# Smaller weight slots, modulation in single k steps with the gates as columns, and transposed rows split and evicted two k tiles at a time, in a three-block float32 layer stack on one core

## The reference, cut to what matters

```python
u = rms_norm(h, norm_g); proj = u @ w_in            # even and odd layer
...
return h + y @ w_out
...
def rms_norm_2(x, g):
    y = xf * lax.rsqrt(jnp.mean(xf * xf, axis=-1, keepdims=True) + EPS)
...
def modulate(h, shift, scale):
    return h * (1 + scale) + shift
```

## Time and profile before

| | before |
|---|---|
| median of 3 runs | 1040.92 us |
| lowest, highest | 1040.67, 1043.06 us |
| profiled execution, its own time | 1042.01 us |
| its span, first to last instruction | 1040.2 us |
| PE busy | 937.6 us (90%) |
| DVE busy | 703.0 us (68%) |
| ACT busy | 475.2 us (46%) |
| mean granted TensorE clock | 0.959 |

### The profile page before, as it was taken

How to read it: one execution, slowest core, us unless ns; L and a number is a source line. 1 busy time by engine, 2 the same in 40 slices (tenths; PEclk the granted TensorE clock), 3 DMA queues, 4 the chain that set the end, 5 groups by cost and what they waited for, 6 DMA issues and landing times. The chain is left out here.

```text
span 1040.2 us, 14368 instructions
## 1 busy us (share of the span) xinstructions
PE 937.6 (90%) x5572; PEld 813.0 (78%) x5572; DVE 703.0 (68%) x1058; ACT 475.2 (46%) x800; POOL 66.9 (6%) x63
## 2 busy tenths in 40 slices
PE   4999988999798899999998989879989489999996
PEld 3788866989677778898988767776678389999885
DVE  4557787878877746757677786658854657754643
ACT  4455644554323335555564534334643434333441
POOL 0201101000000000201020000100001100000000
PEclk8999999899899879999999999989999889999999
DMA  7444364755566455444554575333222437753751
GB/s 266 162 163 145 127 215 161 239 191 187 179 218 217 149 202 163 165 148 158 180 168 142 184 253 194 129 122 122 82 82 81 142 100 243 249 193 108 241 204 41
DMA packets 89348, 174.55 MB, mean 168 GB/s; under 512 B 4269, under 2 KB 8770, under 8 KB 89282
## 3 DMA queue, kind: packets, MB, share of 16 engines
q1 hardware_dynamic: 86656, 166.78, 48.1%
q0 software_dynamic: 1888, 6.25, 1.9%
q10 hardware_dynamic: 738, 0.61, 0.2%
HBM read 172.57 MB, written 1.06 MB: 167 GB/s over the span
## 5 line engine op out<-in xcount | busy, mean ns | idle before, releaser
L1572 DVE TENSOR_TENSOR wlo<-raw,whi 128x1024 fp32r<-128x1024 f32 (+2 forms) x278 | 323.9, 1179 | 149.5 <-ACT whi L1289 148.6
L1289 ACT CAST whi<-raw 128x1024 fp32r<-128x1024 f32 (+2 forms) x278 | 276.7, 1011 | 201.8 <-PE acc L989 71.6
L998 PE MATMUL acc<-xhi,whi 128*128 128x256 f32 x736 | 214.3, 291 | 9.6 <-DVE slo L1590 4.6
L1000 PE MATMUL acc<-xlo,whi 128*128 128x256 f32 x736 | 209.6, 285 | 0.0
L999 PE MATMUL acc<-xhi,wlo 128*128 128x256 f32 x736 | 209.5, 285 | 0.0
L987 PE MATMUL acc<-whi,xhi 128*128 128x512 f32 (+2 forms) x368 | 150.4, 409 | 13.3 <-DVE xlo L1590 6.1
L998 PEld LDWEIGHTS acc<-xhi,whi 128*128 128x128 f32 x736 | 142.5, 194 | 13.0 <-issue 5.3
L989 PE MATMUL acc<-whi,xlo 128*128 128x512 f32 (+2 forms) x368 | 144.0, 391 | 0.0
L988 PE MATMUL acc<-wlo,xhi 128*128 128x512 f32 (+2 forms) x368 | 143.9, 391 | 0.0
L999 PEld LDWEIGHTS acc<-xhi,wlo 128*128 128x128 f32 x736 | 142.5, 194 | 0.7 <-issue 0.5
L1000 PEld LDWEIGHTS acc<-xlo,whi 128*128 128x128 f32 x736 | 142.4, 194 | 0.0
(11 more groups left out here) (291 smaller groups left out, 1175.2 us busy)
## 6 DMA issues: line engine op xcount, KB each, us to landing
raw<-in_e_w_in SPq DMA_DIRECT2D x28, 1024.0 KB, 5.3
raw<-in_o_w_in SPq DMA_DIRECT2D x28, 1024.0 KB, 5.1
raw<-in_w_mod SPq DMA_DIRECT2D x24, 1024.0 KB, 5.1
raw<-in_w_ffn_in SPq DMA_DIRECT2D x20, 1024.0 KB, 5.6
raw<-in_w_in SPq DMA_DIRECT2D x14, 1024.0 KB, 5.2
raw<-in_w_ffn_out SPq DMA_DIRECT2D x10, 1024.0 KB, 5.1
raw<-in_e_w_out SPq DMA_DIRECT2D x8, 1024.0 KB, 5.6
raw<-in_o_w_out SPq DMA_DIRECT2D x8, 1024.0 KB, 5.2
```

The lines of the kernel that those rows point to most:

```text
L998: mm(o, wh, hi, start=a, stop=False, skip_group_check=True)
L1000: last = mm(o, wh, lo, start=False, stop=z, skip_group_check=True)
L1289: nc.scalar.copy(whi[:, s.i % SPLIT_SLOTS, 0:s.nk, 0:n], raw[:, s.raw.i % RAW_SLOTS, s.koff:s.koff + s.nk, 0:n]).then_inc(S["hi_ready"], 1)
L1572: tt(wlo[:, slot, 0:s.nk, 0:n], raw[:, s.raw.i % RAW_SLOTS, s.koff:s.koff + s.nk, 0:n], whi[:, slot, 0:s.nk, 0:n].bitcast(F32), ALU.subtra ...
```

## The change

Raw weights lie in six slots of two k tiles, 512 KB each: the same memory, 326 loads in the place of 164. Modulation takes one k tile per position: one DVE instruction, or two for a ctx chunk, which has them at every second position; the wait for the step before stands at the head of the next. All chunks come out as columns, with the bias from a column; for a gate chunk DVE spreads the four columns over a diagonal (`gate_diag`), and one matmul with ones makes the row (`gate_rows`). The bias loads and `mod_bias` are gone. The chunks move: 0 to 3 now run from sub 12 to sub 82, 4 to 9 from sub 100 to sub 149, 10 and 11 from sub 216 to sub 233, their gate rows at 236 to 240. A sixth and seventh edit lie at the norms: `evac_resid` adds by row tile, with ACT's squares behind each (`mixsq`), so the norms after both layers need no pass over h; at the x norms DVE scales row tile 0 and ACT row tile 1, in two column halves; the 16 transposes come as four quarters of two k tiles, and with modulation ACT makes both xhi and scr from PSUM, DVE only the difference. POOL's load of the memory rows waits for the second raw slot. The memory rows (L1656 now) keep the old way of scaling.

```diff
-RAWK = 4
-RAW_SLOTS, SPLIT_SLOTS, LEAD = 3, 4, 3
+RAWK = 2
+RAW_SLOTS, SPLIT_SLOTS, LEAD = 6, 4, 3
...
-    def transposed(self, xn, ready, key, scale, bias=None):
-        for half in range(2):
-            st = self.step("rows_T", xn=xn, ready=ready, key=key, scale=scale, bias=bias, half=half)
+    def transposed(self, norm, key, scale, bias=None):
+
+        for q in range(4):
+            ready = [(n, norm.on[n] - 1 + q // 2 if norm.both else norm.on[n])
+                     for n in ("rows_ready", "rows_act") if n in norm.on]
+            st = self.step("rows_T", xn=norm.dst, ready=ready, key=key, scale=scale, bias=bias, q=q)
...
+    def mod(self, pos, chunk, ctx=False):
+
+        pos = max(pos, self.pos)
+        stride = 2 if ctx else 1
+
+        def read(k):
+            st = self.step("mod", chunk=chunk, u=k // RAWK, part=k % RAWK, ctx=ctx, prev=self.count.get("mod_read", 0),
+                           after=self.count.get("mod_ps", 0))
             self.tick(st, "mod_read")
...
+        last = pos + (KT - 1) * stride
+        for k in range(KT):
+            self.at(pos + k * stride, lambda k=k: read(k), 3)
+        self.at(last + 2, out, 2)
+        return last + (4 if ctx else 1)
...
-    m = pl.pos
-    for chunk in (6, 7, 8, 9, 0, 1, 2, 3):
-        m = pl.mod(m, chunk, ctx=chunk < 4)
...
+    m = pl.pos
+    for chunk in range(4):
+        m = pl.mod(m, chunk, ctx=True)
...
+    m = max(m, pl.pos + 4)
+    for chunk in range(4, 10):
+        m = pl.mod(m, chunk)
...
-    pl.mod(pl.mod(pl.pos + 4, 4, gate=True), 5, gate=True)
+    assert m <= pl.pos + 4, (m, pl.pos)
+    pl.gate_row(pl.gate_row(pl.pos + 4, 4), 5)
...
-    pl.mod(pl.mod(pl.pos + 8, 10, gate=True), 11, gate=True)
...
+    m = pl.mod(pl.mod(pl.pos + 8, 10), 11)
+    pl.gate_row(pl.gate_row(m + 4, 10), 11)
...
+                if st.both:
+                    wait(("rstd_ready", st.on["rstd_ready"]))
+                    for c in (slice(0, CW), slice(CW, D)):
+                        f(rows_of[st.dst][:, 1, c], rows_of[st.src][:, 1, c], ACT.Copy, scale=stat(st, 2)[:, 1:2])\
+                            .then_inc(S["rows_act"], 1)
+
+            def rows_T(st):
+                hi = (xhi if st.key == "x" else shi)[:, 2 * st.q:2 * st.q + 2, :]
+                wait(("rt_ps", st.on["rt_ps"]))
+                a = scale_cols(st.scale)
+                if st.bias is None:
+                    for k in range(2):
+                        kk = 2 * st.q + k
+                        last = f(hi[:, k, :], acct(st.acc)[:, kk % 4, :], ACT.Copy, scale=a[:, kk:kk + 1])
+                    last.then_inc(S["rt_hi"], 1)
+                    return
+                wait(("mcol_done", st.ready_cols))
+                b = scale_cols(st.bias)
+                tmp = scr[:, st.q % 2 * CW:st.q % 2 * CW + CW].rearrange("p (k t) -> p k t", t=T)
+                for dst in (hi, tmp):
+                    if dst is tmp:
+                        wait(st.free["scr"] if st.q == 0 else ("rt_lo", st.on["rt_lo"] - 2))
+                    for k in range(2):
+                        kk = 2 * st.q + k
+                        last = f(dst[:, k, :], acct(st.acc)[:, kk % 4, :], ACT.Identity, scale=a[:, kk:kk + 1],
+                                 bias=b[:, kk:kk + 1])
+                last.then_inc(S["rt_hi"], 1)
+
+            def evac_resid(st):
+                wait(st.free["scr"])
                 for t in range(NT):
+                    wait(("resid_done", st.on["resid_done"] - 1 + t))
+                    if t == 1:
+                        wait(("sq_ready", st.on["sq_ready"] - 1))
+                    f(scr[:, 0:CW], h_res[:, t, st.c * CW:(st.c + 1) * CW], ACT.Square,
+                      accum_out=mixsq[:, st.c, t:t + 1]).then_inc(S["sq_ready"], 1)
 
...
+            def panels_rstd(st, done):
+
+                wait(("sq_ready", done[0].on["sq_ready"]))
+                link(ts(stat(st, 0)[:, 0:NT], mixsq[:, 0, :], 1.0 / D, EPS, ALU.mult, ALU.add))
+                wait(("sq_ready", done[1].on["sq_ready"]))
+                stt(stat(st, 1)[:, 0:NT], mixsq[:, 1, :], 1.0 / D, stat(st, 0)[:, 0:NT], ALU.mult, ALU.add)\
+                    .then_inc(S["ms_ready"], 1)
+                wait(("rstd_ready", st.on["rstd_ready"]))
+
...
+                dst, src = rows_of[st.dst], rows_of[st.src]
+                if st.both:
+                    for c in (slice(0, CW), slice(CW, D)):
+                        ts(dst[:, 0, c], src[:, 0, c], stat(st, 2)[:, 0:1], None, ALU.mult).then_inc(S["rows_ready"], 1)
+                    return
...
-                b = scale_cols(st.bias)
-                tmp = scr[:, :].rearrange("p (k t) -> p k t", t=T)
-                wait(("rt_ps", st.on["rt_ps"]))
-                wait(st.free["scr"])
-                for k in range(4):
-                    last = ts(tmp[:, k, :], acct(st.acc)[:, k, :], a[:, k0 + k:k0 + k + 1],
-                              b[:, k0 + k:k0 + k + 1], ALU.mult, ALU.add)
-                last.then_inc(S["rt_tmp"], 1)
+                tmp = scr[:, st.q % 2 * CW:st.q % 2 * CW + CW].rearrange("p (k t) -> p k t", t=T)
                 wait(("rt_hi", st.on["rt_hi"]))
                 tt(lo, tmp, hi.bitcast(F32), ALU.subtract).then_inc(S["rt_lo"], 1)
...
-                half = RAWK // 2
-                for k in range(st.part * half, st.part * half + half):
-                    for v in range(2 if st.ctx else 1):
-                        c = scol[:, 8 * v + RAWK * st.u + k:8 * v + RAWK * st.u + k + 1]
-                        src = raw[:, st.raw.i % RAW_SLOTS, k, :]
-                        if st.u == 0 and k == 0:
-                            ins = ts(macc[:, v, :], src, c, None, ALU.mult)
-                        else:
-                            ins = stt(macc[:, v, :], src, c, macc[:, v, :], ALU.mult, ALU.add)
-                        if k % half == half - 1 and v == (1 if st.ctx else 0):
-                            ins.then_inc(S["mod_read"], 1)
-                            wait(("mod_read", st.on["mod_read"]))
-                        elif v == (1 if st.ctx else 0):
-                            link(ins)
-
-            def mod_bias(st):
-                wait(("bias_in", 16 * st.on["bias_in"]))
-                tt(macc[0:1, 0, :], macc[0:1, 0, :], macc[0:1, 1, :], ALU.add).then_inc(S["bias_done"], 1)
-
-            def mod_out(st):
+                wait(("mod_read", st.prev))
+                k = RAWK * st.u + st.part
+                if k == 0:
+                    wait(("mod_ps", st.after))
+                src = raw[:, st.raw.i % RAW_SLOTS, st.part, :]
+                for v in range(2 if st.ctx else 1):
+                    c = scol[:, 8 * v + k:8 * v + k + 1]
+                    m = macc[:, v if st.ctx else st.chunk % 2, :]
+                    if k == 0:
+                        ins = ts(m, src, c, None, ALU.mult)
+                    else:
+                        ins = stt(m, src, c, m, ALU.mult, ALU.add)
+                ins.then_inc(S["mod_read"], 1)
+
+            def mod_take(st):
+                st = st.first
                 wait(("mod_ps", st.on["mod_ps"]))
                 c = st.chunk
-                if st.gate:
-                    which = c >= 6
-                    dve.wait_ge(S["loaded_post_ffn" if which else "loaded_post_mix"], 16)
-                    g = post_gain[which][:, (c % 2) * CW:(c % 2 + 1) * CW]
-                    tt(g, tp[:, :], g, ALU.mult).then_inc(S["mod_sb"], 1)
-                    return
                 for v in range(2 if st.ctx else 1):
                     last = tt(modc[:, v, 4 * c:4 * c + 4], opsum[:, 4 * v:4 * v + 4],
                               cols[:, ROW["b_mod"] + 4 * c:ROW["b_mod"] + 4 * c + 4], ALU.add)
                 last.then_inc(S["mod_sb"], 1)
 
+            def gate_diag(st):
+                c = st.chunk
+                wait(("mod_sb", c + 1))
+                d = macc[:, c % 2, :].rearrange("p (i n) -> p i n", i=4)
+                tt(d, ident.unsqueeze(1).to_broadcast([P, 4, P]),
+                   modc[:, 0, 4 * c:4 * c + 4].unsqueeze(2).to_broadcast([P, 4, P]), ALU.mult).then_inc(S["gate_diag"], 1)
+
+            def gate_rows(st):
+                c = st.chunk
+                dve.wait_ge(S["loaded_post_ffn" if c >= 6 else "loaded_post_mix"], 16)
+                wait(("gate_ps", st.on["gate_ps"]))
+                g = post_gain[c >= 6][:, (c % 2) * CW:(c % 2 + 1) * CW]
+                tt(g, tp[:, :], g, ALU.mult).then_inc(S["gate_sb"], 1)
...
+            def load_mem(st):
+                pool.wait_ge(S["raw_loaded1"], 16)
+                pool.dma_start(h_res[:, :, :], w["mem"].rearrange("b (t p) d -> p (b t) d", p=P))\
+                    .then_inc(S["loaded_h"], 16)
```

More of the change, by code:

```diff
@@ L433, in load @@
         return st
-    def mod(self, pos, chunk, ctx=False, gate=False):
-        pos = max(pos, self.pos) + max(pos, self.pos) % 2
-        def read(u, part):
-            if u == 0 and part == 0 and gate:
```

(52 more changed lines are left out.)

176 lines of the change are left out of this document (97 added, 79 removed).

## The result

| | before | after |
|---|---|---|
| median (4 runs each, beside one another) | 1041.99 us | 1031.51 us |
| lowest, highest | 1040.67, 1045.24 | 1030.55, 1033.49 |
| profiled execution, span | 1042.01, 1040.2 | 1032.34, 1030.5 |
| mean granted TensorE clock | 0.959 | 0.956 |

The account below looks back on a forecast made before the run. TensorE was taken to bound the forgetting heads; elsewhere its waits on DVE's queue and the norm chains, with half-clock spells, were the loss. Terms summed to -32.8: 1042.0 to 1009.2, less 1.1, 1008 us (994 to 1021).

Parts of the forecast that it names:

- The start: Up to the first large matmul: half slots, later memory rows and quartered casts let it issue near 14 us; -5.5 us.
- Windows 205 to 384: Shorter waits for wlo, quartered memory-row transposes, fewer macc instructions and ACT passes: -5, -1, -8 and -1.5 us.
- The squares: Window 610 to 660, mixing half's norm: squares per panel remove ACT's two 1.06 us passes, first sub needs one quarter; -3.5 us.
- The forgetting heads: Window 384 to 547: 45 added macc instructions bring DVE to 88%, costing TensorE some waits; +6 us.
- case A: Rival: added DVE work makes TensorE wait in the forgetting and differential heads, giving most back; 1031 us, chance 0.24.
- Differential heads ... -3: Window 62 to 205: macc pieces of 1.5 us for 3.10 shorten waits, against 6.7 us more DVE load; -3 us.
- The context rows' transposes, in quarters: -1: Window 547 to 610: transposing the context rows in quarters gains 1 us.
- the gate chunks' -5: Window 547 to 610: gate chunks 4 and 5 leave with their bias loads, cutting idle time at macc and bias; -5 us.
- so the sub starts with their end: Norm ahead of the FFN: the first quarter's chain runs beside the other transposes, first sub starts near 834.8; -3.6 us.
- The FFN, -1.7: FFN to the end: the bias waits of `mod_bias` go, -1.5 us, and the last norm loses one DVE instruction, -0.2.
- C: Rival: loads become late, with one in flight in the FFN; 1085 us or more, chance 0.07 shared with another rival.
- D: Rival: clock spells vanish with the gaps in windows 62 to 357 and 547 to 660; 985 us, chance 0.08.

Follow-up runs that it names:

- 12: Changed kernel with POOL's load of the memory rows issued at once, as before the change: 1029.4 us, first large matmul at 15.04 for 15.20.
- 4: Kernel before the change with six slots of 512 KB and nothing else: 1030.3 us, ratio 0.9871 to the kernel before.
- 7: Changed kernel with ACT's passes over h put back at the norms behind both layers, no squares per panel: 1037.9 us, ratio 0.9919.
- 5: Changed kernel with macc steps of chunks 4 to 9, behind each chunk's first, touching one column for 512 (results wrong): 1024.7 us.
- run 1: Changed kernel with column sums placed later, chunk 0 from sub 28 to 31, chunks 1 to 3 to 50, 68 and 86: 1019.0 us, ratio 0.9762.
- 2: Changed kernel with the context rows alone evicted the old way: DVE scales and frees the bank, ACT casts, DVE subtracts: 1030.3 us.
- 6: Changed kernel with column sums later, x norms' first two quarters in score banks, modulated banks freed without DVE's subtraction: 1010.5 us, ratio 0.9668.
- 11: The best kernel: as 6, with context columns made some 20 positions earlier and context rows evicted by DVE, cast by ACT: 1009.0 us, ratio 0.9664.

## Why the prediction was wrong

**Right.** The start (-5.5, measured -5.7), though half of its reason falls: the megabyte of memory rows weighs nothing (12), six slots alone give 1.2 (4), and what is left, the quarters and the split of the first norm, was not run by itself, so the size is in part luck. The first matmul came at 15.2, not near 14. Windows 205 to 384: -15.5 forecast, -21.3 measured. There I credited the gain to macc work that leaves; run 4 shows that 10 of it come from the slots alone. It is argued, not shown, that this is because ACT no longer waits for loads; I had read PE's waits only. The squares (7). The forgetting heads, +3.8 for +6, are right in size by luck: the 3.8 are column sums, which the sum had at nothing, and DVE's load, on which case A rested, costs nothing from sub 100 to 140 (5). DVE is at 81% there (111.14 of 137.6 us), where I had said 88, and PE is never idle. My window of these heads, 384 to 547, reaches into sub 143; with subs 141 and 142 it cost 7.8.

**Wrong, first step: "Differential heads ... -3".** Measured +7.7. I weighed the size of the pieces and the load on DVE, and did not look where the column sums fall. Moved to sub 28, one position behind a pv, they stop TensorE for 6.05 us, and the low clock follows; subs 28 and 29 take 12.3 us more than in run 1. Those at 46 hold the bank for the pv at 47, 2.92 us. With the sums moved again the stretch gives -1.2 and the next one -9.1 for -5.2. Shown by run 1, which also shows what is still lost: ahead of the pv at 31 the sums cost 4.42 us of waiting and 9.0 in three subs, in the best kernel too.

**Second: "The context rows' transposes, in quarters: -1", with the gate chunks' -5.** Measured +8.3, of it 8.8 in subs 140 to 144. I took quarters as earlier in themselves. But a bank half is freed by its second quarter, and ACT's two copies take 3.75 us where DVE's one took 1.90: sub 143 is 4.8 us longer. Runs 2, 6 and 11 take 3.3, 1.6 and 3.4 us back in subs 140 to 144 (with the columns earlier in the last). The other 4.0 us are subs 141 and 142, where the forecast had no sums: those of chunk 8 wait 1.72 us for a macc step, and the clock falls behind them. With light steps 3.5 of the 4.0 go (5), so here DVE's load did cost time, the one place where a run shows case A's cause. In the best kernel 3.6 of the 5.4 us that stay lie there. The gate chunks' leaving gave 0.5 at subs 144 to 160: waits of 2.15 and 3.20 us at subs 156 and 158 became 1.49 and 1.89 at 150 and 153, but a sum at 149 and the gate rows at 153 and 156 now stand between heads.

**Third: "so the sub starts with their end", the FFN norm, -3.6.** Measured +1.2. Same bank, 2.0 us late. Run 6 shows the step as I had written it, 12.9 us from the last matmul of the mixing half (794.46) to the first sub, where I had said 12.5. The bank is less than half of the miss. The rest is the clock at subs 206 and 208, which comes and goes between runs: run 1, with the same code here, has -3.0, and run 6, with the bank mended, -2.6. Its cause stays open.

**The FFN, -1.7.** Measured +0.1; no run was made for it. By the profile, subs 213 to 234 gave the gain (-2.6), and the gate rows of chunks 10 and 11, which the sum had at nothing here, took it back: subs 237 to 241 took 3.3 us more, with a wait of 1.38 us for DVE's diagonal.

```profile
PE tp L1134 <- DVE macc L1882: 1.4, 1, 1.4
```

The three steps fell short by 10.7, 14.3 and 4.8 us, the FFN by 1.8 and the mixing half's norm by 1.3, 32.8 in all; the other stretches gave 9.7 more than forecast, so 23.1 are missing. None of the rivals was this. A has the right time, 1031, by luck and in the main by the wrong cause: runs 1 and 5. C falls: ACT's waits for raw sum to 13.4 us after, where before had 81.2. (D's 985 was also summed wrongly: 20 us less than 1008 is 988.)

The slots also settle the rule I had weighed. The Trainium skill, DMA: Bandwidth & Descriptors, section "Anatomy of one DMA", speaks for transfers of 1 MB by its fixed 2.0 us. That section is on transfers that GpSimd issues; the weights here go by SP. Here 326 loads of 512 KB beat 164 of 1 MB by 1.3% (4). The fixed part is there in the landing times, not on the path; what counted here, as I read the waits above, is when a slot comes free.

## What to carry to other kernels

When a change moves a small step on an in-order engine, ask which buffer it writes, who frees that buffer, and who next waits for it, not only whether its inputs are ready. One position behind a long chain cost 12.3 us here, more than the whole change gained; one position ahead of the next user cost 9.0. Finer pieces help only if the resource they pass through is freed in the same pieces. And before a large edit is written off by its total, sum it by stretches: edits to the placing of sums and the freeing of banks brought 22.5 us more than the 10.5.
